# Modulation vectors 8 and 9 on TensorE and 5 inside the first attention, z products among the compressed branch's turns, gate biases in VectorE's first step

## The chip, the cores and the metric

One NeuronCore of a Trainium2 chip runs the whole program; the metric is the device time of one launch in microseconds (us). Engine names: PE is TensorE, DVE VectorE, ACT ScalarE, POOL GpSimd, and SP the engine whose queue issues the weight transfers.

## What is computed

The input is 256 tokens of 1024 channels in float32. A first block has two layers (an attention with three branches, called nsa, and a dilated attention, dil); a second block has a feed-forward network, a mixer and another feed-forward network. Every layer is modulated by a vector made from a condition `c`:

```python
def adaln_norm(x, c, g, w_ada, b_ada):
    mod = jax.nn.silu(c) @ w_ada + b_ada
    shift, scale, gate = jnp.split(mod, 3, axis=-1)
    h = rms_norm(x, g) * (1.0 + scale[:, None, :]) + shift[:, None, :]
    return h, gate[:, None, :]
...
        x = x + gate * y
```

and in the nsa layer, after `u = h @ w_in`:

```python
        return jax.nn.silu(blk @ w1) @ w2                      # compress(k_c), compress(v_c)
    s_cmp = jnp.einsum('btghd,bngd->btghn', q_plain, k_cmp) * scale
    p_cmp = masked_softmax(s_cmp, cmask[None, :, None, None, :])
    o_cmp = jnp.einsum('btghn,bngd->btghd', p_cmp.astype(v_cmp.dtype), v_cmp)
```

The three branches are weighted, summed, multiplied by `silu(z)` and projected by `w_out`.

## The kernel before

**Weights** stream through a ring of six 512 KB slots (`RING`, tile `ring`). The transfers ("units") have one fixed order, the plan (`Plan`, `first_stages`), and SP issues them in that order: the transfer of unit u waits until unit u-6 was consumed. A unit of a projection is split by ACT into a rounded high part (L528) and by DVE or POOL into a low part (L533), both in `w_parts`; `stream_to` is the code that issues these splits, in plan order, wherever an engine's program calls it, and `stream_end` is a limit on how far it goes. PE multiplies a unit in 12 steps: 8 with the high part (L574, L576) and 4 with the low part (L589), each 512 columns wide; a projection of 512 columns is 4 units, 48 steps.

**Modulation vectors.** Column blocks of 512 of all the modulation matrices are numbered n = 0 to 29, 4 units each. `ada_step(n, kk)` on DVE adds one of the 8 row blocks, weighted by `silu(c)`, to an accumulator (L698 for the first block, L704 for the other seven). `ada_sum` on PE then sums over the partitions: for shifts and scales 4 products of one column (L735); for a gate (n % 6 of 4 or 5, ten of the thirty) 4 products of 128 columns (L740), each followed by a product of 128 columns that adds the bias (L742). `ada_collect` on DVE takes the sums over in order of n, `gate_row` being the gate's result. Vector 3 alone is computed on PE from the ring (`ada_direct`, L757).

**The nsa layer on PE** (`nsa_pe`) goes: projections 2, 3, 0, 1; between them the first products of the compressed branch (`hidden_parts`, L1650, whose weights are the plan's `cmp` units: `in_nsa_ck_w`, `in_nsa_cv_w`); then turns (L651, transposes of q, by PE), the products of the compressed keys and values (L1705, L1710), its scores (L1721), then the z projection (`nsa` 4) in pieces, around the turn of the probabilities and the four products with values (L1735). Then the attention of 32 items in 16 pairs (`Attention.pe`: scores L1167 and L1169, turns of the probabilities L1176, values L1187 to L1189), with steps of the second z projection (`nsa` 5) between, and at last the output projection with the sums of vectors 6 to 9.

**Around it**: DVE rotates q (`rope_parts`, L1302 to L1305), ACT copies it out of the banks, and PE's turns wait for that copy. `Attention.dve` masks scores and calls `beside(i)` for i = 0 to 31, which runs the due `ada_step`s. `turn_probs` waits first for the item's exponentials and then for the copy of an earlier turn.

The places that the change touches, in DVE's program of the nsa layer:

```python
            stream_to("dve", plan.outputs["nsa", 1][1][3])
            ada_collect_up_to(6)
            stream_end["dve"] = plan.outputs["nsa", 1][1][-1]
            rope_parts(dve, ("nsa", 1), lambda tt: gemm_bank("nsa", 1, tt)[:, :], 8)
```

## Time and profile before

| | |
|---|---|
| median of 3 runs | 1240.8 us (1237.46 to 1241.46) |
| the profiled execution | 1239.5 us, its span 1237.7 us |
| mean granted TensorE clock | 0.977 of full speed |
| busy share of the span | PE 92%, DVE 71%, ACT 44%, POOL 12% |

### The profile page before, as it was taken

The page shows a single profiled execution, that of the slowest core. Times are in us where ns is not written, and L with a number is a line of the kernel's source. Part 1 is how long each engine was busy: PE and PEld are TensorE (multiplying, and loading weights), DVE is VectorE, ACT ScalarE, POOL GpSimd, SP SyncE. Part 2 cuts the span into 40 slices and gives each one's busy share as a digit, 9 for nine tenths or more (in the row PEclk, how much of TensorE's full clock was granted, in tenths as well). Part 3 has the DMA queues.
Part 4 walks back from the last instruction along what each step waited for, and adds up shares of the span by engine and source line. Part 5 has one row for each costly group of instructions (what it writes and reads, how often), then busy time and mean ns, then how long its engine had stood idle before and what let it go on. Part 6 is the DMA issues. An engine that isn't in the chain of part 4 may idle for free. (4 is left out here: it accounts for less than half of the span.)

```text
span 1237.7 us, 19929 instructions
## 1 busy us (share of the span) xinstructions
PE 1135.5 (92%) x7662; PEld 954.1 (77%) x7662; DVE 874.1 (71%) x1458; ACT 549.9 (44%) x989; POOL 152.3 (12%) x109
## 2 busy tenths in 40 slices
PE   6878899899898899999989999898988998999997
PEld 5657677777677688888878877787878876888886
DVE  5866798589786699965489946847576656855554
ACT  1333366433363634344477754433141435434542
POOL 0010131122331100000000002104033021000011
PEclk9988899999899999999999999998989999999999
DMA  8875343378654399976455552751102144955452
GB/s 321 288 269 196 112 136 121 109 227 293 219 190 137 106 325 328 342 241 187 153 173 178 169 186 90 249 189 36 37 1 72 59 152 153 318 186 185 160 199 69
DMA packets 143513, 221.63 MB, mean 179 GB/s; under 512 B 10855, under 2 KB 66747, under 8 KB 143291
## 3 DMA queue, kind: packets, MB, share of 16 engines
q1 hardware_dynamic: 140512, 216.37, 53.2%
q10 hardware_dynamic: 2907, 4.00, 0.9%
q8 instruction: 61, 1.00, 0.3%
q14 instruction: 33, 0.27, 0.1%
HBM read 219.28 MB, written 1.05 MB: 178 GB/s over the span
## 5 line engine op out<-in xcount | busy, mean ns | idle before, releaser
L533 DVE TENSOR_TENSOR w_parts<-ring,w_parts 128x1024 fp32r<-128x1024 f32 (+2 forms) x276 | 341.9, 1275 | 90.6 <-ACT w_parts L528 89.8
L528 ACT CAST w_parts<-ring 128x1024 fp32r<-128x1024 f32 (+2 forms) x288 | 290.0, 1036 | 259.6 <-PE bank L576 70.6
L574 PE MATMUL bank<-w_parts,lhs_hi 128*128 128x512 f32 (+2 forms) x960 | 385.2, 402 | 13.6 <-ACT w_parts L528 9.2
L576 PE MATMUL bank<-w_parts,lhs_lo 128*128 128x512 f32 (+2 forms) x960 | 377.2, 393 | 0.0
L589 PE MATMUL bank<-w_parts,lhs_hi 128*128 128x512 f32 (+2 forms) x960 | 266.6, 394 | 18.1 <-DVE w_parts L533 18.1
L589 PEld LDWEIGHTS bank<-w_parts,lhs_hi 128*128 128x128 f32 x960 | 180.4, 191 | 58.8 <-DVE w_parts L533 25.2
L574 PEld LDWEIGHTS bank<-w_parts,lhs_hi 128*128 128x128 f32 x960 | 184.3, 192 | 51.8 <-issue 13.2
L576 PEld LDWEIGHTS bank<-w_parts,lhs_lo 128*128 128x128 f32 x960 | 184.3, 192 | 32.3 <-issue 0.2
L704 DVE SCALAR_TENSOR_TENSOR ada_acc<-ring,c_act,ada_acc 128x512 f32<-128x512 f32 x203 | 168.7, 831 | 13.3 <-DMA ring<-in_ada_w 3.0
L574 PE MATMUL bank<-w_parts,up_hi 128*128 128x512 f32 x176 | 68.7, 390 | 0.0
L576 PE MATMUL bank<-w_parts,up_lo 128*128 128x512 f32 x176 | 68.5, 389 | 0.0
L873 POOL TENSOR_TENSOR x<-x,xn 128x512 f32<-128x512 f32 x10 | 17.6, 1780 | 403.5 <-DVE xn L864 403.5
L651 PE MATMUL bank<-const,arena 128*128 128x128 f32 (+2 forms) x318 | 45.4, 275 | 11.2 <-DVE arena L664 5.1
L651 PEld LDWEIGHTS bank<-const,arena 128*128 128x128 f32 (+2 forms) x318 | 36.7, 141 | 18.9 <-DVE arena L664 5.8
L589 PE MATMUL bank<-w_parts,up_hi 128*128 128x512 f32 x176 | 48.4, 390 | 0.0
L1913 DVE TENSOR_TENSOR arena<-arena,bank 128x256 f32<-128x256 f32 x44 | 17.5, 417 | 39.3 <-ACT arena L1925 39.0
L2031 DVE SCALAR_TENSOR_TENSOR arena<-arena,cols 128x256 f32<-128x256 f32 x96 | 42.2, 481 | 2.3 <-ACT arena L2021 0.8
L1925 ACT ACTIVATE arena<-bank 128x256 f32<-128x256 f32 x44 | 16.3, 382 | 58.8 <-PE bank L589 57.5
L533 POOL TENSOR_TENSOR w_parts<-ring,w_parts 128x1024 fp32r<-128x1024 f32 x12 | 28.9, 2406 | 77.9 <-ACT w_parts L528 77.9
L1244 ACT ACTIVATE arena<-arena 128x128 f32<-128x128 f32 x48 | 19.3, 401 | 43.1 <-DVE arena L1199 40.8
L574 PEld LDWEIGHTS bank<-w_parts,up_hi 128*128 128x128 f32 x176 | 33.0, 188 | 6.8
L576 PEld LDWEIGHTS bank<-w_parts,up_lo 128*128 128x128 f32 x176 | 33.0, 188 | 6.8
(359 smaller groups left out, 1455.6 us busy)
## 6 DMA issues: line engine op xcount, KB each, us to landing
ring<-in_w_ffn_up SPq DMA_DIRECT2D x176, 256.0 KB, 4.2
ring<-in_w_ada SPq DMA_DIRECT2D x72, 512.0 KB, 4.9
ring<-in_ada_w SPq DMA_DIRECT2D x48, 512.0 KB, 4.9
ring<-in_w_ffn_down SPq DMA_DIRECT2D x44, 512.0 KB, 4.6
ring<-in_w_in SPq DMA_DIRECT2D x44, 512.0 KB, 4.5
ring<-in_dil_w_in SPq DMA_DIRECT2D x32, 512.0 KB, 4.6
ring<-in_nsa_w_in SPq DMA_DIRECT2D x20, 512.0 KB, 4.6
ring<-in_w_in SPq DMA_DIRECT2D x20, 416.0 KB, 4.2
```

The costliest lines, as they stand in the source:

```text
L528: eng.copy(hi, raw).then_inc(hi_ready, 1)
L533: eng.tensor_tensor(lo, raw, hi.bitcast(F32), ALU.subtract).then_inc(lo_ready[who], 1)
L574: pe.matmul(b, x_hi, w, start=(k0 + k == 0), stop=False)
L576: mm = pe.matmul(b, x_lo, w, start=False, stop=False)
L589: mm = pe.matmul(bank[2 * plan.pair[o] + tt][:, 0:n], x_hi, lo[:, k * n:(k + 1) * n], start=False, stop=last_k)
L651: mm = pe.transpose(bank_of_turn(i)[0:mout, col:col + kin], src, ident[0:kin, 0:kin])
L704: ins = dve.scalar_tensor_tensor(acc, w, s, acc, ALU.mult, ALU.add)
L873: pool.tensor_tensor(x[:, tt, A_HALF], x[:, tt, A_HALF], y_gated[:, tt, :], ALU.add).then_inc(x_half, 1)
L1244: act.activation(pr[:, 0:P], m[:, 0:P], ACT.Exp, bias=self.bias[:, i, 0:1], scale=SCALE, accum_out=self.den[:, i, 0:1])
L1913: dve.tensor_tensor(up_h[:, j % 2, tt, :], up_a[:, j % 2, tt, :], gemm_bank(name + "_up", j, tt)[:, 256:512], ALU.mult).then_inc(bank_free ...
L1925: act.activation(up_a[:, j % 2, tt, :], gemm_bank(name + "_up", j, tt)[:, 0:256], ACT.Silu).then_inc(silu_done, 1)
L2031: ins = dve.scalar_tensor_tensor(a, p[:, h, tap:tap + T], tap_weight(b, tap, h), a, ALU.mult, ALU.add)
```

## The change

**Order of the weights.** Vector 5's four units leave their place before the `ck` units and go, with those of 8 and 9, between the units of `nsa` 5. The order in which vectors are collected has 5 after 9 (`ADA_ORDER`), and waits that counted collected vectors use `ready_count`.

**Vectors 8 and 9** are computed on PE from the ring, two products of one column ahead of each of the 32 turns in the attention. They go to unused columns of the bank that the turn writes; DVE reads the sums after the attention. `turn_probs` now waits for the earlier copy first, then makes these products, then waits for the exponentials. **Vector 5** takes its 8 DVE steps inside the attention, one at every third call of `beside` from i = 10.

**z products.** Of the 48 steps of `nsa` 4, 12 now stand before the q turns, 12 after them, 12 after the scores of the compressed branch, and the last 12 as 4, 4, 4 around its tail. ACT and DVE split the first two units of `nsa` 4 before they copy or rotate the last projection's q.

**Gate biases.** SP loads the bias of a gate into one partition of a cleared tile (`gate_bias`), ahead of the gate's first unit; DVE's first step of a gate adds it, and PE's sum of a gate is one product of 512 columns.

```diff
-ADA_ON_PE = (3,)
+ADA_ON_PE = (3, 8, 9)
+ADA_ORDER = (0, 1, 2, 3, 4, 6, 7, 8, 9, 5, *range(10, 30))
...
-    s += [gemm("nsa", 0, w, 0, 512, both), ada(5), first_cmp]
+    s += [gemm("nsa", 0, w, 0, 512, both), first_cmp]
...
+    small = (8, 8, 8, 8, 5, 9, 9, 5, 5, 9, 9, 5)
...
+            if kk == 0 and is_gate(n):
+                ins = dve.scalar_tensor_tensor(acc, w, s, gate_bias, ALU.mult, ALU.add)
...
-                    mm = pe.matmul(bank[6][:, c * P:(c + 1) * P], ones, acc[:, c * P:(c + 1) * P],
-                                   start=True, stop=False)
-                    mm = pe.matmul(bank[6][:, c * P:(c + 1) * P], bias_pick(r), rows[0:120, 2, :],
-                                   start=False, stop=True)
+                mm = pe.matmul(bank[6][:, :], ones, acc, start=True, stop=True)
...
+        def ada_direct_product(pe, d):
+            n, i, c = 8 + d // 16, d % 16 // 4, d % 4
+            u = plan.outputs["ada", n][1][i]
+            if c == 0:
+                await_unit(pe, u)
+            for k in range(CHUNKS):
+                kk, at = CHUNKS * i + k, k * 512 + c * P
+                mm = pe.matmul(direct_columns(c % 2)[:, n - 8, c // 2, i:i + 1], ring[:, u % RING, at:at + P],
+                               c_act[:, kk:kk + 1], start=(k == 0), stop=(k == CHUNKS - 1))
...
-                pe.wait_ge(self.exp_done, j + 1)
                 if j >= 2:
                     pe.wait_ge(self.probsT_ready[j % 2], j // 2)
+                if before_turn:
+                    before_turn(j)
+                pe.wait_ge(self.exp_done, j + 1)
...
-            ada_collect_up_to(6)
-            stream_end["dve"] = plan.outputs["nsa", 1][1][-1]
+            stream_end["dve"] = plan.outputs["nsa", 4][1][1]
...
-                some_ada(n_before + (32 - n_before) * (i + 1) // 32 - ada_done[0])
+                some_ada(n_before + min(4, (i + 1) // 2) + max(0, (i - 7) // 3) - ada_done[0])
...
-            some(steps, 24)
-            pe.wait_ge(hidden_act, 1)
-            ada_sum(pe, 5)
             for _ in steps:
                 pass
             hidden_parts(1)
+            steps = gemm_steps(pe, "nsa", 4, from_lhs, "norm0", 512)
+            some(steps, 12)
```

PE's order in the compressed branch, from the products of the compressed values' hidden layer (`ring,arena`) to its scores (128x30 x16). Before, nothing of the z projection stands in it:

```order
L1650 MATMUL bank<-ring,arena 32x256 x16
L651 MATMUL bank<-const,arena 128x128 x8
L1658 MATMUL bank<-const,arena 128x30 x2
L651 MATMUL bank<-const,arena 128x128 x8
L1705 MATMUL bank<-arena 128x30 x2
L1710 MATMUL bank<-arena 120x64 x4
L651 MATMUL bank<-const,arena 128x128 x16
L1721 MATMUL bank<-arena 128x30 x16
```

The same place in the changed kernel, in two pieces (its line numbers are its own: L612, L614 and L627 are the three lines of a z step). First the end of the unit that now stands ahead of the q turns, these turns, and the start of the next unit:

```order
L627 MATMUL bank<-w_parts,lhs_hi 128x512 x4
L689 MATMUL bank<-const,arena 128x128 x8
L1718 MATMUL bank<-const,arena 128x30 x2
L689 MATMUL bank<-const,arena 128x128 x8
L612 MATMUL bank<-w_parts,lhs_hi 128x512
```

Then the end of that unit, the keys and values, the rest of the turns, the scores, and the start of the third unit:

```order
L627 MATMUL bank<-w_parts,lhs_hi 128x512 x4
L1765 MATMUL bank<-arena 128x30 x2
L1770 MATMUL bank<-arena 120x64 x4
L689 MATMUL bank<-const,arena 128x128 x16
L1781 MATMUL bank<-arena 128x30 x16
L612 MATMUL bank<-w_parts,lhs_hi 128x512
```

Two units of z have moved from behind the scores to both sides of the q turns.

PE's order at a pair of items inside the attention, before (scores, a turn, a z step, values):

```order
L1167 MATMUL bank<-arena 128x128 x2
L1169 MATMUL bank<-arena 128x256 x2
L1176 MATMUL bank<-const,arena 128x128 x3
L574 MATMUL bank<-w_parts,lhs_hi 128x512
L1187 MATMUL bank<-arena 128x64
L1188 MATMUL bank<-arena 128x64
L1189 MATMUL bank<-arena 128x64
```

and in the changed kernel:

```order
L1226 MATMUL bank<-arena 128x128 x2
L1228 MATMUL bank<-arena 128x256 x2
L809 MATMUL bank<-c_act,ring 128x1 x2
L1237 MATMUL bank<-const,arena 128x128 x3
L612 MATMUL bank<-w_parts,lhs_hi 128x512
L1248 MATMUL bank<-arena 128x64
L1249 MATMUL bank<-arena 128x64
L1250 MATMUL bank<-arena 128x64
```

Two products with `c_act` (L809) have come ahead of the turn (L1237), and so at each of the 32 turns.

## Rows read from the trace of the kernel before

**Rows 1.** Windows: length, busy us (x records) of PE, PEld, DVE, ACT, POOL, clock, DMA share, GB/s
```profile
75.00:93.00 18.00, 10.77 (x65) 6.89 (x64) 11.12 (x16) 5.29 (x7) 2.53 (x2) 0.81 0.86 291
...
137.00:148.00 11.00, 8.44 (x47) 6.23 (x48) 7.62 (x32) 6.13 (x24) 2.34 (x1) 0.69 0.15 48
```
**Rows 2.** Waits of PE from 60 to 142 us: in total, times, longest
```profile
PE bank L1650 <- DMA ring<-in_nsa_ck_w: 3.9, 2, 2.0
PE bank L651 <- DVE arena L664: 2.5, 1, 2.5
PE bank L574 <- ACT w_parts L528: 2.0, 1, 2.0
PE bank L1658 <- ACT arena L1509: 1.4, 1, 1.4
...
PE bank L651 <- issue: 1.1, 1, 1.1
```
**Rows 3.** Timeline of SP's queue: start us, length us, what
```profile
60.33 3.34 SPq L2846 DMA_DIRECT2D ring<-in_ada_w  x4
68.09 9.71 SPq L2846 DMA_DIRECT2D ring<-in_nsa_ck_w  x4
```
**Rows 4.** Timeline of PE, 76 to 138 us: start, length, what, [idle before <- releaser]
```profile
76.47 1.07 PE L1650 MATMUL bank<-ring,arena 128*32 128x256 f32 x16
...
85.10 0.79 PE L574 MATMUL bank<-w_parts,lhs_hi 128*128 128x512 f32 x1 [1.95 <-ACT w_parts L528]
...
88.68 1.24 PE L589 MATMUL bank<-w_parts,lhs_hi 128*128 128x512 f32 x4
...
92.58 0.48 PE L574 MATMUL bank<-w_parts,lhs_hi 128*128 128x512 f32 x1
```
**Rows 5.** Timeline of PE, 102 to 138 us
```profile
102.80 1.94 PE L1650 MATMUL bank<-ring,arena 128*32 128x256 f32 x32
...
114.50 5.25 PE L1721 MATMUL bank<-arena 128*128 128x30 f32 x32
...
137.29 0.49 PE L1167 MATMUL bank<-arena 64*128 64x128 f32 x4 [0.91 <-ACT arena L1562]
```
**Rows 6.** Timeline of DVE, 109 to 123 us
```profile
109.40 2.36 DVE L533 TENSOR_TENSOR w_parts<-ring,w_parts 128x1024 fp32r<-128x1024 f32 x2 [0.32 <-ACT w_parts L528]
...
122.06 0.73 DVE L1415 TENSOR_TENSOR arena<-arena 128x240 f32<-128x240 f32 x2
```
**Rows 7.** Timeline of PE: prices of small float32 products
```profile
20.00 6.97 PE L757 MATMUL bank<-c_act,ring 128*128 128x1 f32 x32
...
129.11 1.88 PE L1735 MATMUL bank<-arena 120*128 120x512 f32 x4
...
214.46 0.95 PE L735 MATMUL bank<-const,ada_acc 128*128 128x1 f32 x8
215.27 0.49 PE L574 MATMUL bank<-w_parts,lhs_hi 128*128 128x512 f32 x1
```
**Rows 8.** Timeline of PE: a gate's sum in the first feed-forward network
```profile
453.46 0.39 PE L740 MATMUL bank<-ada_acc,const 128*128 128x128 f32 x2
...
455.24 0.60 PE L651 MATMUL bank<-const,arena 128*128 128x128 f32 x4
```
**Rows 9.** Windows: the two feed-forward networks, the first attention
```profile
430.00:550.00 120.00, 120.00 (x598) 101.53 (x597) 106.17 (x143) 51.48 (x68) 0.00 (x0) 1.00 0.92 311
1060.00:1100.00 40.00, 40.00 (x200) 33.78 (x199) 29.41 (x36) 16.70 (x22) 0.00 (x0) 1.00 0.84 280
137.00:203.00 66.00, 57.71 (x446) 47.17 (x447) 56.78 (x202) 42.08 (x152) 18.21 (x11) 0.95 0.35 113
```
**Rows 10.** Timeline of DVE: a first and a later ada step
```profile
328.38 0.49 DVE L698 TENSOR_SCALAR ada_acc<-ring,c_act 128x512 f32<-128x512 f32 x1
328.90 0.75 DVE L704 SCALAR_TENSOR_TENSOR ada_acc<-ring,c_act,ada_acc 128x512 f32<-128x512 f32 x1
```
**Rows 11.** Timeline of PE: a turn of the dilated layer
```profile
323.22 0.66 PE L651 MATMUL bank<-const,arena 128*128 128x128 f32 x4 [1.46 <-DVE arena L664]
```

More of the change, by code:

```diff
@@ L115, with ready_count, summed_count, is_gate @@
 FIRST_CONST = 2 * P + 2
-ADA_ON_PE = (3,)
+ADA_ON_PE = (3, 8, 9)
+ADA_ORDER = (0, 1, 2, 3, 4, 6, 7, 8, 9, 5, *range(10, 30))
+def ready_count(n):
+    return ADA_ORDER.index(n) + 1
+def summed_count(n):
+    return sum(a not in ADA_ON_PE for a in ADA_ORDER[:ready_count(n)])
+def is_gate(n):
+    return n % 6 >= 4
+def ada_source(A, n):
+    layer = min(n // 6, 2)
+    return layer, 512 * (n - 6 * layer)
 class Plan:
@@ L258, in first_stages @@
     s += [gemm("nsa", 2, w, 1024, 512, both), ada(4), kw_gates]
-    s += [gemm("nsa", 0, w, 0, 512, both), ada(5), first_cmp]
+    s += [gemm("nsa", 0, w, 0, 512, both), first_cmp]
     s += [gemm("nsa", 1, w, 512, 512, both), second_cmp]
     s += [gemm("nsa", 4, w, 1792, 512, act), ada(6), ada(7)]
-    s.append(beside([(("nsa", 5), w, 2304)], range(8, 10), 2))
+    big = column_units([(w, 2304, 512)], 512, KC)
+    lots = {n: iter(ada(n)[2]) for n in (5, 8, 9)}
+    small = (8, 8, 8, 8, 5, 9, 9, 5, 5, 9, 9, 5)
+    order, units = [], []
+    for i, unit in enumerate(big):
+        order += [("nsa", 5)] + [("ada", n) for n in small[3 * i:3 * i + 3]]
+        units += [unit] + [next(lots[n]) for n in small[3 * i:3 * i + 3]]
+    s.append(("beside", order, units, act))
     s += [gemm("nsa_out", j, o, 512 * j, 512, gated) for j in range(2)]
@@ L688, in ada_step @@
             acc = ada_acc[:, n % SUMS, :]
-            if n >= SUMS and kk == 0 and n - SUMS not in ADA_ON_PE:
-                dve.wait_ge(ada_summed, n - SUMS + 1 - sum(a < n - SUMS for a in ADA_ON_PE))
+            if kk == 0:
+                earlier = [a for a in range(n % SUMS, n, SUMS) if a not in ADA_ON_PE]
+                if earlier:
+                    dve.wait_ge(ada_summed, summed_count(earlier[-1]))
             k = kk % CHUNKS
@@ L1701, in nsa_pe @@
             turn_tokens(pe, "qp", plain_rows, range(2, 4))
+            some(steps, 12)
             pe.wait_ge(hidden_act, 2)
@@ L1723, in nsa_pe @@
             mm.then_inc(cmp_scored, 1)
-            steps = gemm_steps(pe, "nsa", 4, from_lhs, "norm0", 512)
-            some(steps, 24)
+            some(steps, 12)
             pe.wait_ge(cmp_exp, 1)
@@ L1738, in nsa_pe @@
                 if i % 2:
-                    some(steps, 8)
+                    some(steps, 4)
             await_turns_read(pe, "qr", range(4))
@@ L2843, in _ @@
                         sp.wait_ge({"pe": pe_units, "ada": ada_units}[who], ordinal + 1)
+                if u in plan.gate_at:
+                    n = plan.gate_at[u]
+                    layer, c = ada_source(A, n)
+                    earlier = [v for v in plan.gate_at if v < u]
+                    if earlier:
+                        sp.wait_ge(ada_units, plan.units[earlier[-1]][2] + 1)
+                    else:
+                        sp.wait_ge(bias_cleared, 1)
+                    row = (A["ada_b"][0], A["ada_b"][1], A["b_ada_2"][0])[layer].rearrange("(o c) -> o c", o=1)
+                    sp.dma_start(gate_bias[0:1, :], row[:, c:c + 512]).then_inc(landed[u % RING], 16)
                 for src, kn, width, at, cn in dmas:
```

96 lines of the change are left out of this document (57 added, 39 removed).

## The prediction, made before the changed kernel ran

> **What bounds the kernel now.** I read the busy shares first (PE 92%, every other engine far below), then the windows, then PE's waits and PE's timeline where it waits. The reader is to see two kinds of stretch. In the feed-forward networks PE is busy for 120.0 of 120 us and for 40.0 of 40 at a granted clock of 1.00 [rows 9]: there each microsecond taken off PE is a microsecond of the kernel, as long as the transfers (busy 0.92) and DVE (106 of 120) can follow. In the nsa layer PE waits instead: between 75 and 93 us it is busy for 10.8 of 18 us, at a clock of 0.81 [rows 1]. The reason lies in the order of the weights. SP issues vector 5's four units at 60.33 and the `ck` units only from 68.09 on, over 9.7 us [rows 3], since their slots come free as DVE works through vector 5. PE waits 3.9 us for the `ck` units and then 2.0 us for the next projection's high part [rows 2].
>
> The change acts at five places. I take them in order of time, with minus for a gain.
>
> **1. Up to the compressed values' hidden products.** Without vector 5 ahead of them the `ck` units inherit its slots and its issue times, 60 to 64 us. At the 4.6 us or so that such a transfer takes they have landed before 70 us, while PE asks for them at 76.47 [rows 4]; the first two units of the next projection follow at about 68 us. What PE does from 76.47 to 92.58 [rows 4] is 16.1 us for 16 hidden products, one unit, and ten short ones. At full clock that is 1.9 us (the 16 products at 102.80 [rows 5]), 12 steps of 0.23 us, so 2.75, and 1.2: 5.9 us. So up to 10.2 us go: 3.9 and 2.0 and 1.4 us of waits [rows 2], 1.8 us by which eight z-like steps from 85.10 to 88.68 [rows 4] take 3.6 us in place of 1.8 because the clock had fallen to its half level after the waits, and about 1 us of slow short products. I take 10.0; the lower bound of the gain is the three waits' 7.2 us with a quarter still there, 5.5. Two gate sums stood in this stretch. Vector 5's leaves it: 8 products in 1.78 us by the spacing of such a sum elsewhere, 453.46 to 455.24 [rows 8]. Vector 4's becomes one product of 512 columns; two of these take 1.88 us including the end of the last [rows 7], so one takes 0.86 to 0.94, and the sum gains 0.85 to 0.9. Together **-12.6 us** by the end of the hidden products, which stood at 104.7 [rows 5].
>
> **2. From there to the attention's first scores, 137.29 [rows 5].** The work is the same, in another order. What PE loses there now: 1.1 us that the trace puts down to nothing (by the program it waits for ACT's copies of q), 2.5 us for DVE's copy of a q turn [rows 2] and 0.4 for ACT's, 0.9 us at the end [rows 5], and a stretch at half clock: the 16 score products take 5.25 us [rows 5] where 0.2 us each, the price of row 214.46 [rows 7], makes 3.3, and the eight z steps behind them lose 1.7 more. Together some 8.5 us (1.1, 2.9, 0.9, and 3.6 by the clock). What it will lose: DVE must split the second z unit before it rotates q. That unit's slot comes free only with the last unit of the projection before; with 4.6 us for the transfer and 1.0 and 1.2 us for the two splits, DVE turns to the rotation about 3.3 us after PE has finished the projection, where it turned to it at once. PE covers this with hidden products (1.9) and 12 z steps (2.75), and then still waits some 1.8 us, since rotation and copies take 3.2. DVE's two splits at 109.40, 2.36 us [rows 6], are gone from in front of its copies, which shortens the 2.5 us wait to about 0.9. But behind the scores only 12 z steps, 2.75 us, stand before the turn of the probabilities. DVE reaches the end of the shifted scores 13.4 us after 109.40 now [rows 6], 11.1 without the two splits, and ACT adds 0.7; PE's work in that time is 2.3 us of turns, 3.3 of scores and the 2.75, with 0.9 of wait: a new wait of about 3 us. A wait of 2.5 us [rows 2] had the half clock behind it, so I count one such stretch again, 3.4 us. With the 0.9 at the end and 0.3 for a shorter cover of ACT's copy that is 1.8, 0.9, 3.0, 0.3, 0.9 and 3.4: 10.3. Net **+1.8** (-1.6 if the clock stays up, +5.2 if it falls at the 1.8 us wait too). Then four ada steps (0.75 us each [rows 10]) stand between the last values' copy and the first mask, 2.9 us, where the gap is now 2.9 and will be a PE step or two shorter: **+0.8**.
>
> **3. The attention.** PE gets 64 products of one column whose stationary side is a 128x128 block of the ring. The trace has this price twice: 16 of them in 6.97 us, 0.43 each, at 20 us, and four like them from 214.46 to 215.27, 0.20 each [rows 7]. The first stands in the opening, where every PE product, also those of 512 columns, goes at half the speed that it has later, so I take 0.20: 13.0 us. PE is busy for 57.7 of the 66.0 us from 137 to 203 [rows 9]. If the new work filled each idle moment, the stretch would last 70.7 (+4.7); if none, 79.0 (+13.0). Most of the idle time is waiting for ACT's and DVE's copies of earlier turns; `turn_probs` waits for them before the new products, so they fill only waits for exponentials, but a PE with 4.2 us of work for a pair in place of 3.4 is late for those copies, and DVE loses 8 of its 20 steps there (6.0 us). At the start, with the clock at 0.69 [rows 1], the new products cost 0.4. I take **+9.0**.
>
> The Trainium skill ("TensorE: Matmul & The Clock Gate", section "What happens when you issue a matmul") says that PE can load the next weights while the present product runs. By that rule one of a pair's loads would hide behind the 512-column step ahead of it, and an estimate from the row's 0.2 us for two loads is 0.1 us for each of 32 turns, so 3.2 us less, 1231.1. The four products from 214.46 stand behind such steps too, and their 0.81 us show nothing hidden; I go by the row.
>
> **4. The output projection, and dil.** Two sums of one-column products (0.81 each [rows 7]) leave, one gate product comes: **-0.7**. DVE's two reads of 16 columns and a gate row fall into its idle time there. In dil two gate sums get 0.9 cheaper on PE, but PE waits 1.5 us for a DVE copy behind them [rows 11], and DVE's first step of a gate grows from 0.49 to 0.75 [rows 10], twice: **+0.4**, with -0.9 and +1.0 as bounds.
>
> **5. The feed-forward networks.** Six gate sums, 0.85 to 0.9 each, where PE never waits [rows 9]: -5.2, at least -4 if transfers take some of it. The 2 KB bias transfers ride ahead of a 512 KB unit and wait for a step long past; I count nothing, and if that cover failed, 10 times 0.3 us on SP's queue, +3. Sum here **-5.2**.
>
> **Sum**: -12.6 +1.8 +0.8 +9.0 -0.7 +0.4 -5.2 = -6.5. The profiled execution took 1239.5, which makes 1233.0; it lay 1.3 below the median of the runs, so the forecast is **1234.3**.
>
> **Rivals.**
> - *The opening's gain is kept and PE swallows the new products* (chance 0.22): part 2 at -1.6, the attention at +6 (which hidden loads alone would do). That gives -12.6 -1.6 +0.8 +6.0 -0.7 +0.4 -5.2 = -12.9, 1228. For it: 8.3 us of idle PE in the attention. Against: the wait of 3 us is new and the row that is like it had the half clock behind it.
> - *The gain is taken back further on* (0.15): part 2 at +5.2 and the attention at +11 leave -1.1: 1239.7. For it: each of PE's waits in the attention hangs on a chain from exponentials to turn to copy, which PE's extra work lengthens.
> - *Slower, by the price of the new products* (0.10): if they cost 0.43 each as in row 20.00 [rows 7], the attention grows by 27.5 less the 4 us of idle time that I let them fill, +23.5 in place of +9.0: -6.5 becomes +8.0, 1249. Slower by over 3.7 us begins at 0.36 us a product. For it: that row is the same operation. Against: its neighbours were slow too.
> - *The order of the weights does nothing* (0.02): PE still waits for `ck`, and the new costs stay: +3.5, 1244.
>
> **How the numbers follow.** My forecast (-3 to -11) has 0.51. 0.3%, 3.7 us, is about what a measurement of this kernel can tell from no change. Faster by more: 0.22, and 0.51 less the 0.02 of its edge: 0.71. Within it: the edge and 0.14 of the second rival, 0.16. Slower: 0.01 of the second, 0.10 and 0.02: 0.13. The range leaves out the two last rivals and the far end of the first, so it goes from 1226 (rival one with a dil stage at -0.9 and the opening at its full 10.2) to 1241.5 (rival two with the networks at -4).
>
> **What would show it.** Right: no PE wait for `ck` at 76 us and none for the projection behind it; hidden products of the values done near 92 us; a PE wait of about 3 us before the turn of the probabilities with the half clock behind; first attention scores at 124 to 127; some 75 us of attention with PE busy for over 90% of it; `c_act` products at 0.2 us; gate sums of 0.9 us. Wrong: c_act products at 0.4 us, an attention under 71 or over 80 us, or transfers of z that arrive later than 5 us after their slot is free.

## The result, and the profile after

The changed kernel takes 1268.8 us (median of 4 runs: 1276.5, 1275.4, 1258.0, 1262.2) against 1241.0 for the kernel before, measured beside it: a ratio of 1.0224, 95% interval 1.013 to 1.032. It is slower by 28 us, where 6.5 us faster was forecast, and the time lies far outside the range. The four runs spread over 18 us; the kernel before spreads over 4 here. The profile is that of the slowest of the four. Where the runs of a kernel below lie apart like this, each run's time is given, since no median says what they did.

The first lines of the page of the changed kernel (a digit is a slice of 32 us; PEclk is the granted clock in tenths):

```profile
span 1274.7 us, 19847 instructions
...
PE   6898999998979989999999999989898898999997
...
DVE  5867334468979669997548975675767657765554
...
PEclk9998555599989999999999999998999999999999
```

Read the clock's line before any other. Four slices, 127 to 255 us, stand at 5, which is half speed, with PE at 9 above them and DVE at 3 and 4, below its usual 6. That is the attention of the nsa layer. The windows of the changed kernel, with the columns of [rows 1]:

```profile
75.00:93.00 18.00, 18.00 (x133) 13.40 (x132) 9.32 (x13) 8.52 (x11) 2.55 (x2) 1.00 0.70 237
...
123.00:131.00 8.00, 3.29 (x21) 2.27 (x22) 7.05 (x19) 3.36 (x11) 2.37 (x1) 0.87 0.43 131
131.00:253.00 122.00, 122.00 (x553) 106.76 (x553) 47.52 (x182) 42.58 (x143) 15.80 (x10) 0.50 0.24 76
```

The first row is the stretch where PE waited in [rows 1]: 18.0 us busy of 18 in place of 10.8, so the opening went as forecast. The last is the attention: 122 us, PE busy in all of them, the clock at 0.50 (1.2 of 2.4 GHz) in all of them. Busy share alone would call this stretch perfect.

PE's waits in the changed kernel from 60 to 140 us, against [rows 2] (in total, times, longest):

```profile
PE bank L1226 <- DVE arena L1281: 3.9, 1, 3.9
PE bank L689 <- issue: 1.5, 1, 1.5
PE bank L1226 <- ACT arena L1621: 0.9, 1, 0.9
PE bank L689 <- DVE arena L702: 0.6, 1, 0.6
PE bank L612 <- ACT w_parts L566: 0.3, 1, 0.3
```

The waits for `ck` and for the projection behind it are gone. One is new, 3.9 us for the first masks of the attention. PE's timeline there, and one later pair:

```profile
90.72 1.93 PE L1710 MATMUL bank<-ring,arena 128*32 128x256 f32 x32
...
123.79 0.49 PE L1226 MATMUL bank<-arena 64*128 64x128 f32 x4 [0.90 <-ACT arena L1621]
124.09 0.63 PE L1228 MATMUL bank<-arena 64*128 64x256 f32 x4
128.64 0.63 PE L1226 MATMUL bank<-arena 64*128 64x128 f32 x4 [3.92 <-DVE arena L1281]
129.05 1.07 PE L1228 MATMUL bank<-arena 64*128 64x256 f32 x4
130.05 1.01 PE L809 MATMUL bank<-c_act,ring 128*128 128x1 f32 x4
130.93 0.88 PE L1237 MATMUL bank<-const,arena 128*128 128x128 f32 x3
...
133.98 0.80 PE L1226 MATMUL bank<-arena 64*128 64x128 f32 x4
...
141.94 0.80 PE L1226 MATMUL bank<-arena 64*128 64x128 f32 x4
```

L1710 is the products of [rows 5] at 102.80, now 12.1 us earlier. From one pair's scores to the next it takes 7.96 us (133.98 to 141.94). What DVE and POOL did in the 3.9 us:

```profile
122.61 0.48 DVE L740 TENSOR_SCALAR ada_acc<-ring,c_act 128x512 f32<-128x512 f32 x1
123.12 4.35 DVE L746 SCALAR_TENSOR_TENSOR ada_acc<-ring,c_act,ada_acc 128x512 f32<-128x512 f32 x3
127.40 0.28 DVE L1279 CUSTOM_DVE_ANT_0 arena<-bank,const 128x128 f32<-128x128 f32 x1
```
```profile
124.56 2.37 POOL L571 TENSOR_TENSOR w_parts<-ring,w_parts 128x1024 fp32r<-128x1024 f32 x1 [26.93 <-ACT w_parts L566]
```

Three steps of 0.75 us took 4.35: POOL's 2.37 us split of a z unit lies inside them. The first mask waits behind, and PE for it.

Aligned at the same places of the program (starts of the lines' first or last product), the changed profile against the one of before stands so:

| up to | before, us | after, us | this part gained (-) or lost | forecast |
|---|---|---|---|---|
| the attention's first scores | 137.3 | 123.8 | -13.5 | -10.8 |
| its last value product | 202.5 | 252.9 | +63.9 | +9.8 |
| first product of layer 0's norm | 234.5 | 283.6 | -1.3 | -0.7 |
| the same after dil | 408.3 | 455.6 | -1.8 | +0.4 |
| the same after the first network | 614.6 | 658.1 | -3.8 | -3.5 |
| the same after the mixer | 1029.4 | 1068.3 | -4.6 | 0 |
| last product of the second network | 1230.3 | 1267.3 | -1.9 | -1.7 |

One part is wrong by 54 us; the rest gained more than forecast. Differences of one or two microseconds between two profiles mean little: over the kernel before and its three variants below, dil takes 167.5 to 173.8 us and the second network 198.8 to 200.9.

### The profile page after: what moved, and what is told of

It reads as the page before. It is cut to its first block and busy times, and to the rows that moved or that the text cites. A ratio compares the mean times of both kernels' runs of the same rounds, so it can differ in the third digit from the quotient of the medians.

```text
span 1274.7 us, 19847 instructions
## 1 busy us (share of the span) xinstructions
PE 1188.5 (93%) x7634; PEld 999.9 (78%) x7634; DVE 862.1 (68%) x1444; ACT 552.2 (43%) x989; POOL 152.7 (12%) x110
## 5 line engine op out<-in xcount | busy, mean ns | idle before, releaser
L571 DVE TENSOR_TENSOR w_parts<-ring,w_parts 128x1024 fp32r<-128x1024 f32 (+2 forms) x276 | 342.0, 1276 | 89.6 <-ACT w_parts L566 88.7
L612 PE MATMUL bank<-w_parts,lhs_hi 128*128 128x512 f32 (+2 forms) x960 | 387.9, 404 | 10.7 <-ACT w_parts L566 6.1
L614 PE MATMUL bank<-w_parts,lhs_lo 128*128 128x512 f32 (+2 forms) x960 | 379.9, 396 | 0.0
L627 PE MATMUL bank<-w_parts,lhs_hi 128*128 128x512 f32 (+2 forms) x960 | 267.1, 394 | 18.0 <-DVE w_parts L571 18.0
L627 PEld LDWEIGHTS bank<-w_parts,lhs_hi 128*128 128x128 f32 x960 | 181.0, 191 | 57.9 <-DVE w_parts L571 24.6
L612 PEld LDWEIGHTS bank<-w_parts,lhs_hi 128*128 128x128 f32 x960 | 185.1, 193 | 48.9 <-issue 14.2
L614 PEld LDWEIGHTS bank<-w_parts,lhs_lo 128*128 128x128 f32 x960 | 185.4, 193 | 32.8 <-issue 1.0
L746 DVE SCALAR_TENSOR_TENSOR ada_acc<-ring,c_act,ada_acc 128x512 f32<-128x512 f32 x189 | 155.2, 821 | 13.5 <-DMA ring<-in_ada_w 3.5
L612 PE MATMUL bank<-w_parts,up_hi 128*128 128x512 f32 x176 | 68.7, 390 | 0.0
L614 PE MATMUL bank<-w_parts,up_lo 128*128 128x512 f32 x176 | 68.5, 389 | 0.0
L689 PE MATMUL bank<-const,arena 128*128 128x128 f32 (+2 forms) x318 | 46.0, 279 | 10.8 <-ACT arena L702 4.0
L702 DVE COPY arena<-bank 128x384 f32<-128x384 f32 (+1 forms) x33 | 19.5, 592 | 53.5 <-PE bank L1237 47.5
L627 PE MATMUL bank<-w_parts,up_hi 128*128 128x512 f32 x176 | 48.4, 390 | 0.0
L809 PEld LDWEIGHTS bank<-c_act,ring 128*128 128x128 f32 x128 | 31.4, 327 | 10.5 <-issue 9.8
L612 PEld LDWEIGHTS bank<-w_parts,up_hi 128*128 128x128 f32 x176 | 33.0, 188 | 6.8
```

What stands on the lines that cost most here:

```text
L571: eng.tensor_tensor(lo, raw, hi.bitcast(F32), ALU.subtract).then_inc(lo_ready[who], 1)
L612: pe.matmul(b, x_hi, w, start=(k0 + k == 0), stop=False)
L614: mm = pe.matmul(b, x_lo, w, start=False, stop=False)
L627: mm = pe.matmul(bank[2 * plan.pair[o] + tt][:, 0:n], x_hi, lo[:, k * n:(k + 1) * n], start=False, stop=last_k)
L689: mm = pe.transpose(bank_of_turn(i)[0:mout, col:col + kin], src, ident[0:kin, 0:kin])
L702: return eng.tensor_copy(dst, src) if eng is nc.vector else eng.copy(dst, src)
```

## The experiments

**Theory A**: the 64 one-column products keep the clock down. Once it has fallen, here by the 3.9 us wait, an attention that holds them can't bring it back, perhaps because PE spends part of each pair loading weights for a single column. **Rivals**: the wait alone decides; the products let the clock fall by themselves (Theory B below); the attention is long for a reason other than the clock (C); or any added work does it, whatever its width (A2).

**masks_first**: the wait taken away.

```diff
-            some_ada(CMP_ADA[2])
...
-                some_ada(n_before + min(4, (i + 1) // 2) + max(0, (i - 7) // 3) - ada_done[0])
+                some_ada(n_before + min(8, i) + max(0, (i - 7) // 3) - ada_done[0])
```

> The changed kernel with one edit: VectorE's four multiply-adds of the modulation vectors that stood between the compressed values' copies and the attention's first mask are done one by one behind the first masks instead. The changed kernel's profile shows a TensorE wait of 3.9 us there, the granted clock at 0.50 from then to the end of the attention (129 us long, 123.8 to 252.9), where the kernel before is back at 1.00 within 10 us. Theory A (the wait starts it, and the one-column products keep the clock down): without the wait of 3.9 us the clock stays at 1.00 through the attention, which then takes about 75 us, and the kernel takes some 54 us less than the profiled 1274.7: about 1222. Theory B (the mix of the attention with one-column products brings the clock down by itself, the wait only came first): the clock still falls within the attention, and at least 30 us of the 54 stay lost: 1250 or more. Theory C (the length of the attention has another cause than the clock): the clock may rise but the attention keeps over 100 us.

Measured: 1220.8, 1274.4, 1228.0 and 1278.7 us. The wait for the masks shrank to 1.3 us as meant, and the kernel has two times. The 1220.8 us run is the profiled one; its attention:

```profile
123.00:139.00 16.00, 14.38 (x72) 11.93 (x73) 9.14 (x34) 7.49 (x28) 2.34 (x1) 0.60 0.22 67
139.00:199.50 60.50, 59.67 (x504) 52.20 (x502) 43.43 (x164) 34.93 (x124) 15.86 (x10) 0.99 0.45 143
```

The clock fell here too, after waits of 0.9 and 1.3 us, but came back at 139, and then stayed. The two runs near 1276 have a mean clock of 0.93, that of the changed kernel's slowest. So the long wait isn't needed for the bad time, and neither A nor B holds as put: whether the clock comes back differs from run to run of one program. C is out, since with the clock up the attention takes 76.1 us. At full clock the products cost what was forecast:

```profile
150.01 0.48 PE L627 MATMUL bank<-w_parts,lhs_hi 128*128 128x512 f32 x1
150.33 0.50 PE L809 MATMUL bank<-c_act,ring 128*128 128x1 f32 x4
150.69 0.53 PE L1237 MATMUL bank<-const,arena 128*128 128x128 f32 x3
...
152.91 0.61 PE L809 MATMUL bank<-c_act,ring 128*128 128x1 f32 x4
153.38 0.53 PE L1237 MATMUL bank<-const,arena 128*128 128x128 f32 x3
```

From the start of a pair of products (four records) to the turn behind it: 0.36 us behind a 512-column step, 0.47 behind scores, so about 0.2 each. At half clock the same took 0.88 (130.05 to 130.93 above).

**quarter_direct**: the wait stays, three quarters of the products go.

```diff
-            for k in range(CHUNKS):
+            for k in range(CHUNKS) if c == 3 else ():
```

> The changed kernel with three quarters of its one-column products left out (of the four columns of vectors 8 and 9 only the last one is computed, so the modulation values of these two vectors are not the reference's); all waits and all else stay, the 3.9 us wait before the attention too. Theory A: with 16 products spread over every fourth turn the clock falls at the wait but comes back early in the attention, within about 15 us, as it does in the kernel before; the attention takes about 72 us and the kernel about 1217. The rival (the products do not matter, the clock falls by the wait and the attention cannot lift it in this kernel at all, for instance since its z products are as thin as before): the clock stays at 0.50 to the attention's end, which takes 129 less 48 x 0.44 = 108 us: about 1253.

Measured: 1208.6 to 1218.8 in four runs, median 1215.9. With the same 3.9 us wait the clock is back at 131:

```profile
123.00:131.00 8.00, 3.80 (x21) 2.60 (x22) 6.95 (x21) 2.84 (x10) 2.37 (x1) 0.80 0.43 131
131.00:188.00 57.00, 54.84 (x457) 46.69 (x455) 45.25 (x177) 39.16 (x142) 15.92 (x10) 1.00 0.48 152
```

The wait alone is out.

**before_late_steps**: VectorE's four steps put ahead of the first mask in the kernel before, without products.

```diff
-            some_ada(CMP_ADA[2])
             for i in range(4):
...
+            some_ada(CMP_ADA[2])
```

> The kernel before with one edit: VectorE's four multiply-adds that stand before the compressed values' copies are moved behind them, so that they stand between these copies and the first mask, as in the changed kernel. No one-column products here. Theory A: TensorE waits some 2 to 4 us more for the first masks, the clock falls as it did or a little earlier, and is back at 1.00 within 10 to 15 us of attention: the kernel takes 1240 to 1247. The rival (the wait alone decides, whatever the attention consists of): the clock stays at 0.50 for most of the attention, which takes over 95 us in place of 65: 1270 or more.

Measured: 1238.5 us, ratio 0.999 (0.997 to 1.001), ten runs from 1234.7 to 1244.0, a little below the 1240 expected. VectorE's steps in this place cost nothing there, but the run doesn't test what it was meant to: the longer wait didn't come. In its profile PE waits 1.3 us for the first masks, as in the kernel before. POOL's split starts at 141.79 there, when the three steps that began at 139.44 are done (2.39 us in place of 4.35). The wait alone is ruled out by quarter_direct, not by this run.

**before_gate_bias**: the third part of the change alone, on the kernel before (the edit is that part of the diff above).

> The kernel before with one part of the change alone: the gate biases are added in VectorE's first step of a gate vector, and a gate's column sum on TensorE is one product of 512 columns in place of eight of 128. By the prediction each of the ten gate sums saves 0.85 to 0.9 us on TensorE, six of them in the feed-forward networks where they count in full: -5 to -8 us in all, 1233 to 1236. The changed kernel gained 13.5 us between its attention's end and the end of the kernel where -5.5 was predicted; if the gate biases are the cause of that surplus, this kernel gains 12 us or more: 1229 or less. If it gains nothing, the transfers or the longer first step eat the gain.

Measured: 1235.6 us, ratio 0.9974 (0.9949 to 0.9999), so -3.2 us with an interval of -6 to 0. The forecast was -5 to -8: the gain is smaller, though the interval reaches into it.

**wide_columns**: is it the width? The products keep weights, places and number, and move 64 columns.

```diff
-                mm = pe.matmul(direct_columns(c % 2)[:, n - 8, c // 2, i:i + 1], ring[:, u % RING, at:at + P],
-                               c_act[:, kk:kk + 1], start=(k == 0), stop=(k == CHUNKS - 1))
+                mm = pe.matmul(bank[2 + c % 2][:, 3 * P + 16:3 * P + 80], ring[:, u % RING, at:at + P],
+                               ident[:, 0:64], start=(k == 0), stop=(k == CHUNKS - 1))
```

> The changed kernel with one edit: each of the attention's 64 one-column products keeps its weights (the same block of the ring) but moves 64 columns of the identity in place of one column of the conditioning vector, so that vectors 8 and 9 are not computed. The wait of 3.9 us before the attention stays, so the clock falls there. Theory A1 (what holds the clock down is that these products leave the array nearly empty while weights are loaded): with 64 columns the clock comes back to 1.00 within some 15 us in every run, the attention takes 75 to 80 us and the kernel 1220 to 1226, with no run above 1235. Theory A2 (any work of this length between the turns does it, by stretching the pairs or by its weight loads, whatever the columns): the clock stays at 0.50 for most of the attention as in the changed kernel, in some or all runs: 1255 to 1280.

Measured: 1215.4 to 1222.3 in four runs, median 1220.0. The same number of weight loads, more work for PE, the same 3.9 us wait, and 49 us less. In its profile, from 131 us on:

```profile
131.00:200.00 69.00, 67.59 (x556) 59.23 (x555) 47.75 (x182) 39.62 (x142) 15.89 (x10) 0.97 0.40 126
```

A2 is out. Beside the number of columns, what is moved (the identity) and where the results go are different too; copies_64 below takes the first of these back.

**late_direct** and **masks_first_late**: no products in the first 8 of 32 turns, so that the attention starts as densely as before.

```diff
+        def late_direct(pe, j):
+            t = (j - 8) // 2
+            for m in range(16 * t // 12, 16 * (t + 1) // 12) if j >= 8 else ():
+                ada_direct_product(pe, 2 * m + j % 2)
...
-    small = (8, 8, 8, 8, 5, 9, 9, 5, 5, 9, 9, 5)
+    small = (8, 5, 8, 8, 8, 5, 9, 9, 5, 9, 9, 5)
...
```

> The changed kernel with its 64 one-column products kept out of the first 8 of 32 turns and spread over the other 24 (one or two pairs of them ahead of a turn), and one unit of vector 5 loaded earlier so that the ring follows. The wait of 3.9 us stays. Theory A: in the first 8 turns the attention is as dense as in the kernel before, so the clock is back at 1.00 within 10 to 15 us, and in masks_first's profile the attention with all products held 1.00 from 140 to 200 once it was there; so the clock stays up, the attention takes about 76 us and every run lies at 1215 to 1226. The rival (at full clock the mix also lets it fall, by chance of the moment): some runs lie above 1240.

> Both edits together: masks_first (VectorE's four steps behind the first masks) and late_direct (no one-column product in the first 8 turns). masks_first alone gave 1220.8, 1228.0, 1274.4 and 1278.7: its wait is 1.3 us and the clock fell all the same, and came back in two of four runs. Theory A: with dense first turns it comes back in all: 1212 to 1222 in every run, a ratio of 0.98 to 0.985 to the kernel before. If the four steps that VectorE now does among the first masks cost as much as the wait did: no faster than late_direct.

Measured: late_direct 1259.2, 1222.6, 1261.0, 1246.1; masks_first_late 1263.3, 1254.5, 1268.5, 1223.0, 1263.4, 1266.9. Both were expected below 1226 in every run; both missed. The profile of late_direct shows why:

```profile
131.00:155.00 24.00, 23.26 (x193) 19.56 (x193) 19.22 (x71) 15.35 (x60) 4.86 (x3) 0.99 0.35 111
155.00:233.00 78.00, 78.00 (x358) 69.51 (x358) 29.14 (x106) 26.40 (x84) 10.97 (x7) 0.50 0.26 86
```
```profile
151.95 1.05 PE L809 MATMUL bank<-c_act,ring 128*128 128x1 f32 x8 [0.69 <-ACT arena L702]
152.87 0.52 PE L1242 MATMUL bank<-const,arena 128*128 128x128 f32 x3
...
154.13 0.95 PE L809 MATMUL bank<-c_act,ring 128*128 128x1 f32 x8
154.94 0.64 PE L1242 MATMUL bank<-const,arena 128*128 128x128 f32 x3
```

The clock was up from 131, as expected. Then one wait of 0.69 us and two turns with twice the products (eight records each), and at 155 it fell, to stay down for 78 us. So Theory A must be widened: the products don't only keep the clock down, with them it can fall from full speed at a wait that the kernel before bore in its profile. That kernel's waits of PE from 148 to 200 us, at a clock of 1.00 throughout:

```profile
PE bank L1176 <- ACT arena L664: 4.1, 6, 1.6
PE bank L1176 <- DVE arena L664: 1.3, 3, 0.5
```

The doubled pairs aren't needed. In the profile of masks_first_late the clock is 1.00 from 131 to 144 us; then the first pair of products comes behind a wait, a single pair follows, and from 145 to 238 the clock is 0.52:

```profile
142.72 0.61 PE L809 MATMUL bank<-c_act,ring 128*128 128x1 f32 x4 [1.33 <-ACT arena L702]
144.46 0.60 PE L809 MATMUL bank<-c_act,ring 128*128 128x1 f32 x4
144.92 0.88 PE L1242 MATMUL bank<-const,arena 128*128 128x128 f32 x3
```

Nor is the fall certain: masks_first's good run had a wait of 0.7 us among its products and kept its clock.

**masks_first_half**: half the products (vector 9 alone), vector 8 back on VectorE.

```diff
-ADA_ON_PE = (3, 8, 9)
+ADA_ON_PE = (3, 9)
...
-    small = (8, 8, 8, 8, 5, 9, 9, 5, 5, 9, 9, 5)
+    small = (9, 8, 8, 8, 9, 8, 5, 9, 5, 5, 9, 5)
...
```

> masks_first with vector 8 given back to VectorE: TensorE has 32 one-column products, two ahead of every second turn, and VectorE 20 steps in the attention as in the kernel before. Theory A with half the dose: quarter_direct (16 products) came back within 10 us in all four runs, the full dose in two of four with the masks first, so half of it should come back in nearly all: 1212 to 1225. If VectorE's extra eight steps (6.0 us) lengthen the attention more than the 6.5 us of products that TensorE is spared, it is no faster than masks_first_late.

Measured: 1229.5 to 1259.8 in six runs, median 1238.5, where 1212 to 1225 was expected. The order of units was badly chosen: PE waits 5.1 us for vector 9's second unit and the clock falls behind that wait; in the profile it comes back at 189 us, after some 45 us, with half the products in place. That fits a half dose, but the new wait blurs it.

**copies_64**: the width as a remedy, with nothing left out. The same column is moved 64 times by a broadcast operand; results go to ascending columns, so that each product's copies are written over by the next.

```diff
+            col = 3 * P + 8 * (n - 8) + 2 * i + c // 2
...
-                mm = pe.matmul(direct_columns(c % 2)[:, n - 8, c // 2, i:i + 1], ring[:, u % RING, at:at + P],
-                               c_act[:, kk:kk + 1], start=(k == 0), stop=(k == CHUNKS - 1))
+                mm = pe.matmul(bank[2 + c % 2][:, col:col + 64], ring[:, u % RING, at:at + P],
+                               c_act[:, kk:kk + 1].broadcast_to([P, 64]), start=(k == 0), stop=(k == CHUNKS - 1))
```

> The changed kernel, whole, with one edit: each of the 64 products of vectors 8 and 9 moves the same column of the conditioning vector 64 times (a broadcast operand) in place of once. The results go to ascending columns of the bank, so each product's first column stays and its 63 copies are written over by the next ones. Vectors 8 and 9 are computed. The wait of 3.9 us stays. Theory A1 (a nearly empty array at each weight load is what holds the clock down): as wide_columns, which gave 1215 to 1222 in four of four runs: 1214 to 1224, attention about 76 us, clock back at 1.00 within 15 us. The rival (wide_columns came back by something else than its width, for instance by other operands or banks): some runs at 1240 to 1280.

Measured: 1216.3 to 1224.3 in four runs, median 1221.2, ratio 0.985 (0.982 to 0.988). The width of 64 products turns 28 us slower into 18 us faster. Its attention:

```profile
131.00:134.00 3.00, 3.00 (x22) 2.33 (x21) 1.43 (x4) 2.24 (x9) 0.00 (x0) 0.84 0.00 0
134.00:198.00 64.00, 62.60 (x531) 55.08 (x530) 45.30 (x173) 37.13 (x133) 15.87 (x10) 1.00 0.41 135
```

**copies_16** (16 in place of 64) and **copies_112**:

> As copies_64 with 16 copies in place of 64. Theory A1 says only that it lies between one column (1258 to 1276) and 64. If the width counts in proportion, 16 copies add a quarter of what 64 add, and some runs should stay at half clock for a part of the attention: median 1225 to 1260 with a spread of 20 us or more. If the spread is as small as with 64 (under 10 us), little width is enough.

> copies_64 with 112 copies per product. If 64 already keeps the clock up in every run, more width brings nothing and costs what the wider product takes: 0 to 4 us more than copies_64 (64 products, at most 48 more columns each), 1221 to 1226. If the clock still lingers at half level after the 3.9 us wait with 64, it comes back sooner and the two are equal.

Measured: with 16 copies 1276.9, 1276.4, 1227.8, 1227.7; with 112 copies 1226.4, 1226.7, 1221.8, 1221.2. With sixteen columns two runs of four are bad, the profiled one from end to end:

```profile
123.00:252.00 129.00, 125.08 (x572) 108.79 (x572) 53.76 (x199) 45.03 (x152) 18.17 (x11) 0.52 0.25 81
```

With 64 and with 112 it came back in every run. 112 brings nothing more: its ratio to the kernel before is 0.986 (0.984 to 0.989), the same as that of copies_64 within what the runs can tell.

Counted over all versions with the 64 products of the change: of the 18 runs with one column (changed kernel, masks_first, late_direct, masks_first_late) 14 took over 1245 us; of the 22 with 64 or 112 columns (wide_columns, the copies of 64 and 112, masks_first_copies, copies_64_old_gates) none took over 1229.

**masks_first_copies**: both remedies.

> copies_64 and masks_first together: VectorE's four steps behind the first masks, and 64 copies per product. masks_first had a wait of 1.3 us in place of 3.9 before the attention, and its runs were 1221 to 1279 by the clock; with the width the clock should come back in all of them. Theory A1: 1211 to 1219 in every run, 2 to 4 us less than copies_64 (the 2.6 us of wait, and up to a few us of half clock), ratio to the kernel before about 0.98. Rival: the attention's speed is set elsewhere by then and it equals copies_64 within 2 us.

Measured: 1218.2 us (1217.2 to 1224.0, four runs), ratio 0.984 (0.981 to 0.986). The fastest whole version tried; 3 us below copies_64, which is within what these runs can tell.

**before_products**: the suspected cost by itself, on the kernel before.

```diff
+                for i in range(2 if self.steps == 16 else 0):
+                    pe.matmul(bank[2 + j % 2][:, 3 * P + i:3 * P + i + 1], ident, c_act[:, i:i + 1], start=True, stop=True)
                 for b in range(3):
                     mm = pe.transpose(bank[2 + j % 2][:, b * P:(b + 1) * P],
```

> The kernel before with 64 one-column products added and nothing else changed: two ahead of each of the attention's 32 turns, with the identity as weights and a column of the conditioning vector moving, into columns that nobody reads. The output is the reference's. This is the suspected cost by itself, without the new order of weights, vectors 5, 8 and 9 and the gate biases. In the kernel before the clock falls by three short waits at 137 to 142 us and comes back at 147. Theory A: with the products it does not come back, or falls again, in most runs: the attention takes 100 to 129 us in place of 65 and the kernel 1270 to 1305, with a spread of over 20 us. The rival (the products cost only their time of 0.21 us each at full clock, and it is the changed kernel's other edits, its longer wait above all, that bring the clock down): 5 to 13 us more than before, 1244 to 1254, with no run above 1260.

Measured: 1249.0, 1249.8, 1252.8 and 1297.6. Three runs pay 10 to 13 us, the products' own time; one pays 58, at a mean clock of 0.93. So the products can bring the half clock with no other edit (the slow run has no profile; its mean clock says it), but Theory A expected it in most runs and it came in one of four. The profiled run, 1249.0 us, holds 1.00 from 135 to 200 us through waits of 1.3 and 1.1 us. In the changed kernel the other edits seem to make it likelier, though four runs of each say little. Which of them, beside the wait, wasn't tried; the products' weights differ as well, the identity here and a new block of the ring there.

**copies_64_old_gates**: the gate biases taken back.

```diff
...
-                mm = pe.matmul(bank[6][:, :], ones, acc, start=True, stop=True)
+                for c in range(4):
+                    r = 4 * n + c
+                    mm = pe.matmul(bank[6][:, c * P:(c + 1) * P], ones, acc[:, c * P:(c + 1) * P],
+                                   start=True, stop=False)
+                    mm = pe.matmul(bank[6][:, c * P:(c + 1) * P], bias_pick(r), rows[0:120, 2, :],
+                                   start=False, stop=True)
...
```

> copies_64 with the gate part of the change taken back: VectorE's first step of a gate vector is the plain product again, TensorE adds each gate's bias by its own products (eight of 128 columns for a gate), no bias transfers. If the gate biases are worth what the prediction said (ten sums, 0.85 to 0.9 us each, less about 1 us of VectorE's and transfers' cost): 5 to 8 us more than copies_64's 1221.2, 1226 to 1229. If they are the whole of the surplus seen after the attention (13.5 us): 1231 or more. If the gain lies in the order of the weights: within 2 us of copies_64.

Measured: 1227.6 us (1226.5 to 1228.9, six runs) against copies_64's 1221.2, 6.4 us more. The two were measured at different times, each beside the kernel before; by their ratios to it, 0.989 and 0.985, the gate biases are worth 5.5 us, give or take 4. In its profile the first network takes 206.2 us as before (206.3), in copies_64's 202.4: four gate sums, 0.95 us each.

**masks_first_half_copies**: half the products, widened, vector 9's units loaded earlier.

> masks_first_copies with vector 8 given back to VectorE, so 32 products of 64 copies ahead of every second turn, and the units loaded in an order in which vector 9's second unit comes earlier than in masks_first_half (where TensorE waited 5.1 us for it). With the clock up TensorE has 6.5 us less work in an attention where it is busy nearly all the time; VectorE has 6 us more. If TensorE bounds the attention: 4 to 6 us less than masks_first_copies' 1218.2, 1212 to 1214. If VectorE's steps and the copies behind them bound it by then: equal within 2 us or slower.

Measured: 1227.0 us (1223.6 to 1231.3, six runs), 9 us more than masks_first_copies (6 by the ratios, 0.988 and 0.984), where 4 to 6 less was hoped for. Another 3.7 us wait of PE for vector 9's unit, and an attention of 80.5 us against 73.2. The clock fell at that wait and stayed down for more than 20 us, in an attention whose products are all 64 columns wide:

```profile
150.00:155.00 5.00, 5.00 (x23) 3.87 (x22) 1.53 (x4) 2.00 (x9) 1.03 (x1) 0.50 0.00 0
...
172.00:175.00 3.00, 3.00 (x28) 2.56 (x27) 1.84 (x7) 2.80 (x10) 0.00 (x0) 1.00 0.71 256
```

So width doesn't make an attention safe from a long wait in its middle; the clock did come back by itself. My order of units failed twice; whether half the products with a good order would win stays open.

## Why the prediction was wrong

**Part 1 was right.** -12.6 forecast, -12.1 measured (90.72 against the 102.80 of [rows 5]); no wait for `ck`, the hidden products done at 92.6 where "near 92" was written.

**Part 2, the turns.** +1.8 forecast, -1.4 measured. The 3 us wait before the turn of the probabilities did not come: the half clock came ahead of it, with the 16 score products (5.09 us against the 5.25 of [rows 5]), and PE was slow enough not to wait. In the profile of wide_columns, where the clock was 1.00 from 106 to 112 us, the scores took 3.65 us and the wait came, 2.5 us, though no half clock behind it (the next z steps are 0.23 us apart). The last term was mis-sized: four ada steps before the first mask, +0.8 forecast. They took 4.35 us for three of them, since POOL's split ran at the same time, and cost 2.7 us (4.85 us from the first to the second scores, 2.18 in the kernel before). The trace of before has such a collision at the attention's start (POOL's split of 2.34 us from 138.06, and inside it a DVE step on 4 columns that takes 0.98 us, 0.17 in the changed kernel), and I did not look for one here. The Trainium skill ("SBUF — State Buffer", section "SBUF: two separate sides") says that a VectorE operation with two SBUF inputs and a GpSimd operation that reads SBUF exclude each other for a whole instruction; 4.35 less 2.25 is 2.1 us, close to the 2.37 of the split, so the trace agrees.

**Part 3 is the step that failed.** Its price was right: 0.20 us a product forecast, 0.18 to 0.23 measured at full clock. The lower figure is behind a 512-column step, so about 0.1 us a pair does seem to hide there, where I read that nothing was hidden; the mean of the two kinds of turn still gives 13.3 us for the 32 turns. Its sum was right as well, at full clock: +0.8 and +9.0 forecast over the attention's 65.2 us, 74.8 in copies_64 (+9.6), 73.2 in masks_first_copies. What failed is the assumption that stands in one half sentence, "At the start, with the clock at 0.69 [rows 1], the new products cost 0.4", which takes the recovery of the kernel before, by 148 us, as given. I treated the clock as a state the products would meet; it is a state that they help to set. The attention took 129.1 us, 54.3 more than copies_64's with the same wait, the same number of products and the same order: that is the clock in the profiled run, and it is more than the whole of the miss. I had half clocks as terms of 3.4 us in part 2, where dense z steps follow; I didn't ask what follows in the attention.

The trace of before held a warning that I passed over. I took the 16 products at 20.00 [rows 7] for slow because their neighbours were slow too. But PE is busy from 14.70 to 32.13 us there, 17.4 us in which 70 of the 81 records of its products are of one column, all at half speed; and once 512-column steps come, at 39.66, they are at full speed within 9 us, a wait of 1.5 us included:

```profile
28.56 3.57 PE L757 MATMUL bank<-c_act,ring 128*128 128x1 f32 x16
...
40.65 0.63 PE L574 MATMUL bank<-w_parts,lhs_hi 128*128 128x512 f32 x1
41.08 0.63 PE L576 MATMUL bank<-w_parts,lhs_lo 128*128 128x512 f32 x1
...
48.30 0.39 PE L574 MATMUL bank<-w_parts,lhs_hi 128*128 128x512 f32 x1
48.53 0.39 PE L576 MATMUL bank<-w_parts,lhs_lo 128*128 128x512 f32 x1
```

The steps start 0.43 us apart at 40.65 and 0.23 apart at 48.30, the two levels of the clock. (The granted clock of the windows reads 1.00 for this whole opening, so there only the distances tell.) No run shows that the narrow products are what held the opening at half speed, but the row called for the question.

The rival "slower, by the price of the new products" had the right sign for another reason. Each product did cost 0.44 us, but so did everything around it: a pair took 7.96 us. My bound counted the price on 64 products only and could not reach past 1249.

The Trainium skill ("TensorE: Matmul & The Clock Gate", section "What's actually happening") says that the clock follows how busy the engine has recently been. The runs agree that what the engine does decides it, but not if busy means the profile's busy share: 122.00 of 122 us busy at 0.50, and 54.84 of 57 at 1.00 in quarter_direct.

**Parts 4 and 5.** The output projection -1.3 for -0.7; dil -1.8 where the bounds were -0.9 to +1.0, but that stage differs by 6 us between profiles of the same code, so this says nothing; the two networks -5.7 for -5.2 (0.95 a sum in the first, 0.85 to 0.9 forecast). The gate biases as a whole are worth 5.5 us (1 to 10) by copies_64_old_gates and 3.2 (0 to 6) on the kernel before. One slip in the range: its upper end, rival two with the networks at -4, adds up to 1240.9 and not 1241.5. The mixer's -4.6 is unexplained. All profiles with the new order of vectors show it (408.2 to 412.0 us from norm to norm, 409.6 with the old gate sums too), none of the kernel before and its variants does (413.1 to 415.5), so it isn't the gate biases; I found no cause.

**What stays open**: how the width of the products acts on the clock (that it does is shown, by what isn't); why some runs of one program recover and others don't; which edit besides the wait, if any, makes the changed kernel fall more often than before_products.

## What to carry to other kernels

Before filling a busy PE's gaps with products of one column, ask what the clock does there, and look at the clock's line first when time is lost at a busy share of 1. Here such products cost 8 to 13 us by their own time and, in the worst runs, some 54 more by the half clock for all around them. Widening them by a broadcast operand costs little (0.39 to 0.49 us a pair with 64 columns, 0.36 to 0.47 with one) and is worth trying wherever weights are loaded for a few columns; times of one kernel that lie far apart, with a lower mean clock in the longer ones, are the sign to look for.

## What the runs showed of the hardware

I hadn't expected that PE can be busy for 122 us without a gap and never leave the half clock, nor that 64 columns per weight load in place of one ends that here (none of 22 runs), with 16 in between (two runs of four). The price of the wider product at full clock, in copies_64:

```profile
152.22 0.48 PE L627 MATMUL bank<-w_parts,lhs_hi 128*128 128x512 f32 x1
152.53 0.55 PE L810 MATMUL bank<-c_act,ring 128*128 128x64 f32 x4
152.92 0.50 PE L1238 MATMUL bank<-const,arena 128*128 128x128 f32 x3
```

Two products of 64 columns take 0.39 us from start to the turn behind, where two of one column take 0.36: the 63 further columns of each are nearly free.
